# A two-layer transformer on one core: first recurrent products inside the expert merge, and gelu in two buffer pairs

## The reference, cut to what matters

```python
y = ys[dest] * flat_w[order][:, None]            # two experts for each token
xl = xl + gt2 * segment_sum(y, tok)              # the merge, layer 0
hl = modulate(rmsnorm(xl, norm_g[1, 0]), sh1, sc1)
yl, ul = split(hl @ w_in + b_in, 2)              # the recurrent mixer, layer 1
ul = centred_dwconv(ul, conv_w, conv_b)          # 4 taps along the positions
for d in range(2):                               # both directions
    r, ig = sigmoid(ul @ w_gate[d, 0] + ..), sigmoid(ul @ w_gate[d, 1] + ..)   # block-diagonal, 4 blocks
    log_a = LRU_C * r * log_sigmoid(lam[d])
    h_d = scan(exp(log_a), sqrt(-expm1(2 * log_a)) * ig * ul)
out = (gelu(yl) * (h_0 + h_1)) @ w_o + b_o
```

## Time and profile before

| | us |
|---|---|
| median of 3 runs | 2863.82 |
| the profiled execution, as timed | 2864.9 |
| its span in the trace | 2863.1 |
| merge, from the first gather to the last copy | 1578.8 to 1658.4 |
| recurrent stage, first product to the projection's first | 1664.8 to 2082.5 |
| TensorE busy | 2596.7 (91% of the span) |
| VectorE, ScalarE, POOL busy | 1089.8, 858.5, 476.7 |

### The profile page before, as it was taken

How to read it: one execution, slowest core, us unless ns; L and a number is a source line. 1 busy time by engine, 2 the same in 40 slices (tenths; PEclk the granted TensorE clock), 3 DMA queues, 4 the chain that set the end, 5 groups by cost and what they waited for, 6 DMA issues and landing times. The chain is left out here.

```text
span 2863.1 us, 68691 instructions
## 1 busy us (share of the span) xinstructions
PE 2596.7 (91%) x28050; PEld 1802.8 (63%) x28051; DVE 1089.8 (38%) x2482; ACT 858.5 (30%) x1860; POOL 476.7 (17%) x590
## 2 busy tenths in 40 slices
PE   7999999999899689999999489999999599999990
PEld 6888788887645357777776344444445477777770
DVE  3234433443553622222222636556465322222225
ACT  3222322232310023333333514334310133333333
POOL 0111211121221022222222300000010122222222
PEclk9999999999999789999999589999999699999995
DMA  6323223232533397999998610000233799999995
GB/s 255 118 95 112 102 95 120 84 111 73 215 134 139 140 413 313 416 416 395 416 416 327 208 60 30 29 29 29 89 133 125 320 410 417 416 417 416 416 376 180
DMA packets 128661, 644.58 MB, mean 225 GB/s; under 512 B 18865, under 2 KB 31441, under 8 KB 72609
## 3 DMA queue, kind: packets, MB, share of 16 engines
q1 hardware_dynamic: 94912, 540.05, 47.7%
q0 software_dynamic: 17984, 57.16, 5.6%
q10 hardware_dynamic: 15648, 45.71, 4.1%
HBM read 578.29 MB, written 64.57 MB: 225 GB/s over the span
## 5 line engine op out<-in xcount | busy, mean ns | idle before, releaser
L1362 PE MATMUL PS<-wt,xT 128*32 128x256 f32 x13056 | 751.5, 381 | 32.2 <-DVE xT L1500 19.1
L1362 PEld LDWEIGHTS PS<-wt,xT 128*32 128x32 f32 x13056 | 512.4, 110 | 231.8 <-issue 40.6
L1377 PE MATMUL PS<-wt,hidT 128*32 128x256 f32 x6528 | 395.2, 379 | 3.5 <-ACT y L1270 3.5
L1270 ACT ACTIVATE y<-PS 32x256 f32<-32x256 f32 x816 | 305.6, 375 | 304.4 <-PE PS L1377 295.7
L1500 DVE STREAM_TRANSPOSE xT<-xg 128x256 f32<-128x256 f32 x206 | 91.8, 446 | 670.1 <-PE PS L1362 653.7
L1377 PEld LDWEIGHTS PS<-wt,hidT 128*32 128x32 f32 x6528 | 256.7, 110 | 99.4 <-issue 4.4
L719 PE MATMUL PS<-hT,slab 128*128 128x256 f32 x1280 | 295.3, 385 | 6.3 <-DVE low L612 3.5
L719 PEld LDWEIGHTS PS<-hT,slab 128*128 128x128 f32 x1280 | 239.3, 192 | 42.6 <-issue 6.5
L432 POOL TENSOR_SCALAR prob<-prob,inv 128x640 f32<-128x640 f32 (+2 forms) x80 | 130.1, 1626 | 661.3 <-DVE inv L627 661.3
L1218 POOL DMA_INDIRECT xg<-h_d,ib x212 | 207.6, 979 | 166.8 <-POOL ib L1215 166.8
L510 ACT ACTIVATE prob<-prob,low 128x640 f32<-128x640 f32 (+2 forms) x160 | 117.6, 735 | 300.3 <-DVE low L612 300.2
(11 more groups left out here) (234 smaller groups left out, 2637.7 us busy)
## 6 DMA issues: line engine op xcount, KB each, us to landing
wt<-in_w SPq DMA_DIRECT2D x256, 1024.0 KB
wt<-in_w2s SPq DMA_DIRECT2D x128, 1024.0 KB
aw<-in_ada_w SPq DMA_DIRECT2D x48, 1024.0 KB, 5.1
ys_d<-y ACTq DMA_DIRECT2D x204, 128.0 KB
slab<-in_slabs SPq DMA_DIRECT2D x24, 512.0 KB, 3.4
tab<-in_tables SPq DMA_DIRECT2D x8, 1408.0 KB, 7.2
ys_d<-zero POOLq DMA_DIRECT2D x4, 2560.0 KB, 9.5
x_d<-x_p ACTq DMA_DIRECT2D x18, 512.0 KB, 5.0
```

Of the source, the lines that this page charges most:

```text
L1270: ins = a.activation(y[rows, q * QD:q * QD + QD], PS[STRIP * q:STRIP * q + STRIP, DOWN, 0:QD], ACT.Copy)
L1362: mm = t.matmul(PS[32 * g:32 * g + 32, UP, 0:QD], xT[:, k * 32:k * 32 + 32], wt[b][:, q, c * 1024 + g * QD:c * 1024 + g * QD + QD], start= ...
L1377: mm = t.matmul(PS[32 * g:32 * g + 32, DOWN, 0:QD], hT_[:, k * 32:k * 32 + 32], wt[b][:, q, c * 1024 + g * QD:c * 1024 + g * QD + QD], sta ...
```

## The change

1. In the recurrent stage `y2` and `yb` become two buffers each, one for each half. `gelu_in(b,o)` waits for the `close` two halves back, and for half 1 the tanh moves behind `gates(b,1,0)`. The loops over b are written out, with fixed indices. Waits and semaphore increments that only served the loops go.
2. Block 0's product of `wu` leaves the recurrent stage and is made in the merge, over pairs of tiles: after an odd tile n TensorE multiplies both halves with the 256 columns of tiles n-1 and n. `SA` and `SB` are collected there, so that the turns have only PSUM banks 6 and 7, one pair.
3. The copies to `hT` are shared anew. An even tile is copied by both engines, four blocks each; an odd tile by ScalarE alone, eight blocks. VectorE's copies of an even tile stand behind the `norm` of the next tile.
4. `x2` gets a third buffer, and ScalarE touches Sqrt once ahead of the first `weigh`.
5. `wu`, `wy` and `wg` of block 0 are loaded when the slot of the last expert but one is free. The five small vectors are loaded right after the twelve loads of the first experts, and the constants of lambda are made on ScalarE and VectorE ahead of the first item; so are `scol` and `gcol`.

The last merge moves into a class `MergeEnd` with the same instructions, apart from a first Sqrt as in 4.

```diff
+            def into_third(self, sp):                        # MergeMid; expert 30's slot is free
+                self.lru.load_wu(sp, 0)
+                self.lru.load_wy(sp, 0)
+                self.lru.load_wg(sp, 0)
+            def before_items_vector(self, v):
+                v.wait_ge(self.vec_in, 80)
...
+                once(v.tensor_scalar(flat(r.bg), flat(r.bg), 0.5, None, ALU.mult))
+            def evac(n):                                     # ScalarE
+                a.wait_ge(self.tr_ok, n + 1)
+                for k in range(KD if n % 2 else KD // 2):
+                    ins = a.activation(self.hT[:, k, n * P:(n + 1) * P], banks(6, 2)[:, k * P:(k + 1) * P], ACT.Identity,
...
+            def turn(n):                                     # TensorE
+                t.wait_ge(self.dg_ok, 2 * n + 2)
+                t.wait_ge(self.eva_ok, n)
+                t.wait_ge(self.evv_ok, (n + 1) // 2)
+                for k in range(KD):
+                    mm = t.matmul(banks(6, 2)[:, k * P:(k + 1) * P], self.x2[n % 3][:, k * P:(k + 1) * P], self.diag[n % 2][:, :],
...
+            def product(n):
+                t.wait_ge(self.eva_ok, n + 1)
+                t.wait_ge(self.evv_ok, (n + 2) // 2)
+                cols = slice((n - 1) * P, (n + 1) * P)
+                for o in range(2):
+                    for k in range(KD):
+                        t.matmul(banks(3 * o, 3)[:, cols], self.lru.wu[:, k, o * P:(o + 1) * P], self.hT[:, k, cols],
+                                 start=(k == 0), stop=(k == KD - 1))
+            turn(0)
+            t.wait_ge(self.lru.wu_in, 16)
+            for n in range(NT):
+                if n + 1 < NT:
+                    turn(n + 1)
+                if n % 2:
+                    product(n)
...
+            for n in range(NT):                              # VectorE
+                if n + 1 < NT:
+                    add(n + 1)
+                norm(n)
+                if n % 2:
+                    evac(n - 1)
@@ experts, SP @@
+                    merge.early_loads(sp)                    # the five vectors, behind 12 weight loads
                     sp.wait_ge(tab_ok, 1)
@@ recurrent, ScalarE @@
-                            a.wait_ge(z_ok, n + 1)
-                            a.activation(yb[:, :], banks(6, 2), ACT.Identity, bias=bin_[:, 0, k]).then_inc(y_ok, 1)
+                        if n >= 2:
+                            a.wait_ge(z_ok, n - 1)
+                        a.activation(yb[o][:, :], banks(6, 2), ACT.Identity, bias=r.bin[:, 0, k]).then_inc(y_ok, 1)
...
+                        gelu_in(b, 1)
+                        gates(b, 1, 0)
+                        gelu_tanh(b, 1)
+                        gates(b, 1, 1)
@@ recurrent, TensorE @@
+                    t.sem_inc(u_ps, 2)
+                    for b in range(LB):
+                        if b:
+                            t.wait_ge(r.wu_in, 16 * b + 16)
...
+                            product(wu, 1, SB, N, u_ps)
```

More of the change, by code:

```diff
@@ L51 @@
 LW = 1024
+CONV = 4
 LB = 4
@@ L1079, in experts @@
+        def experts(l, nt, w_in, merge):
             dst, w01 = tabs
             NA = 2 * nt
-            last = hT is None
             small = Place(nc, SMALL_AT, RING_AT)
@@ L1128, in experts @@
             passed, sp_passed = nm("passed"), nm("sp_passed")
-            nm = lambda s: sem(f"{s}_c{l}")
-            ys_ok, cols_in, cols_ok, rows_in, x_in = nm("ys_all"), nm("cols"), nm("cols_ok"), nm("rows"), nm("x_in")
-            turned = nm("cols_turned")
-            y_in = [gather_sem(f"y_in{j}_c{l}") for j in range(2)]
-            x_out = [nm(f"x_out{j}") for j in range(2)]
-            ya_ok, s_ok, m_ok, x2_ok, sum_ok, sqrt_ok = (nm(x) for x in ("ya", "ysum", "gated", "x2", "sum", "sqrt"))
-            rs_ok, dg_ok, tr_ok, eva_ok, evv_ok, ob_ok = (nm(x) for x in ("rs", "diag", "turned", "ev_act", "ev_dve", "ob"))
+            ys_ok = nm("ys_all")
+            merge.begin(ys_ok, y)
             iot, tok = cst[:, C_IOT:C_IOT + ITEMS], cst[:, C_TOK:C_TOK + nt]
@@ L1325, in _ @@
                     t.matmul(PS[:, 0, 0:w], ltri[:, :], flat(A2), start=False, stop=True).then_inc(summed, 1)
-                    if not last:
-                        t.wait_ge(cols_in, 48)
-                        t.matmul(PS[:, 5, 0:4 * KD], y[0:4 * KD, 0:P], ident[0:4 * KD, 0:4 * KD], start=True, stop=True
-                                 ).then_inc(turned, 1)
+                    merge.early_tensor(t)
                     e32 = slice(0, EXPERTS)
@@ L1414, in _ @@
                     t.sem_inc(used[5], DEEP - 1)
-                    if not last:
-                        for n in range(nt):
-                            j = n % 2
-                            t.wait_ge(dg_ok, n + 1)
-                            if n >= 2:
-                                t.wait_ge(eva_ok, n - 1)
-                                t.wait_ge(evv_ok, n - 1)
-                            for k in range(KD):
-                                mm = t.matmul(banks(2 * j, 2)[:, k * P:(k + 1) * P], x2[j][:, k * P:(k + 1) * P], diag[j][:, :],
-                                              start=(k % 4 == 0), stop=(k % 4 == 3))
-                            mm.then_inc(tr_ok, 1)
+                    merge.tensor(t)
                 @block.vector
@@ L1520, in _ @@
                             hidden(n)
-                    if not last:
-                        v.wait_ge(turned, 1)
-                        v.wait_ge(cols_in, 48)
-                        for w in range(2):
-                            c = 2 * KD * w
-                            v.tensor_copy(scol[:, w, :], PS[:, 5, c:c + KD]).then_inc(cols_ok, 1)
-                            v.scalar_tensor_tensor(out=gcol[:, w, :], in0=PS[:, 5, c + KD:c + 2 * KD], scalar=1.0, in1=ncol[:, :],
-                                                   op0=ALU.add, op1=ALU.mult).then_inc(cols_ok, 1)
-                        v.wait_ge(cols_ok, 4)
@@ L1551, in norm @@
-                    def norm(n):
-                        j = n % 2
-                        v.wait_ge(sqrt_ok, n + 1)
-                        if n >= 2 and not last:
-                            v.wait_ge(dg_ok, n - 1)
-                        v.reciprocal(rs[:, j:j + 1], rt[:, j:j + 1]).then_inc(rs_ok, 1)
-                        v.wait_ge(rs_ok, n + 1)
-                        if last:
-                            if n >= 2:
-                                v.wait_ge(x_out[j], 16 * (n // 2))
-                            v.scalar_tensor_tensor(out=ob[j][:, :], in0=x2[j][:, :], scalar=rs[:, j:j + 1],
-                                                   in1=fin[:, :], op0=ALU.mult, op1=ALU.mult).then_inc(ob_ok, 1)
-                        else:
-                            if n >= 2:
-                                v.wait_ge(tr_ok, n - 1)
-                            v.tensor_scalar(diag[j][:, :], ident[:, :], rs[:, j:j + 1], None, ALU.mult).then_inc(dg_ok, 1)
@@ L1568, in evac @@
-                    def evac(n):
-                        j, w = n % 2, 0 if n < NTL else 1
-                        v.wait_ge(tr_ok, n + 1)
-                        for k in range(KD // 2, KD):
-                            ins = v.tensor_scalar(hT[:, k, n * P:(n + 1) * P], PS[:, 2 * j + 1, (k - 4) * P:(k - 3) * P],
-                                                  gcol[:, w, k:k + 1], scol[:, w, k:k + 1], ALU.mult, ALU.add)
-                        ins.then_inc(evv_ok, 1)
-                    add(0)
```

902 lines of the change are left out of this document (517 added, 385 removed).

## The result

The changed kernel takes 2823.05 us (median of four runs, 2815.8 to 2824.55) against 2863.42 us for the kernel before: a ratio of 0.985, 95% interval 0.984 to 0.987, or 40 us less. Five further runs of the same kernel, taken later as an experiment, gave 2816.4 us (0.985, 0.983 to 0.986). The nine together do not scatter about one value: five lie from 2815.0 to 2817.1, four from 2822.2 to 2824.6, and none between. That gap turned out to be the most instructive part of the case. The profiled execution took 2824.55 us (span 2822.8), so it is one of the upper group.

What follows compares the result with a forecast made beforehand. TensorE was taken to bound the recurrent stage outside its stops, and the merge to leave it about 3 us free per tile. Terms: -30.2 - 23.5 + 3.5 + 3.0 + 0.5 = -46.7 us, forecast 2817.5 us, range 2808 to 2830.

Steps and rivals of the forecast that it cites:

- Part 1: Recurrent stage, stop before each block's last two gate products: two y2/yb buffers remove four stops, -30.2 us.
- Parts 2 and 3: Merge and recurrent stage's start: wu's product moves into a longer merge; gates start at 1691.9 instead of 1715.4, -23.5 us.
- Part 4: Merge, four TensorE gaps of about 3.0 us: one or two clock falls, +3.5 us, ends 0 and 9.6.
- the dear end: Merge gaps: the clock falls in all four, making the clock term 9.6 us instead of 3.5.
- The first rival: Merge: the clock falls in every gap, +6 us, 2823.5 us; chance 0.15.
- Part 5: Before the first item: VectorE waits for vectors queued behind 12 loads, first item 3.0 us late; ends 0 and 7.
- Part 6: End of the items: loads of wu, wy, wg may share DMA engines with the last store, +0.5 us, ends 0 and 3.
- No stop stayed: Rival, recurrent stage: another wait replaces z_ok and the stops stay, +30 us, 2847.5 us; chance 0.07.
- stay at the low clock: Rival, merge: TensorE stays at 1.2 GHz throughout, merge some 44 us later, 2858 us; chance 0.02.
- the slower case: Rival, expert items: moved loops slow their products; 4.1% growth cancels the gain, 7% gives 2898 us; chance 0.03.

## Why the prediction was right, and where it was not

The forecast was 2817.5 us in a range of 2808 to 2830. The first four runs' median is 2823.05, the median of all nine is 2817.07. The mechanisms of parts 2, 3 and 5 were right and that of part 1 half told; that the sum came so close is in part luck, as the steps show:

**Part 1, -30.2.** Measured -30.3 in the stage and -31.8 with this part alone. The sum was right, its cause only half told. The text gave the stop to the one `y2`/`yb` pair and named the Tanh's place in a subordinate clause. The kernels with one pair and with the Tanh ahead show two edits of about equal worth: with the pair alone the stop is 2.40 us, with the Tanh behind the gates alone 3.08. The tail after the last gates stayed hidden, as costed: the projection follows at 2042.21 without a break.

**Parts 2 and 3, -23.5.** From the merge's first gather to the first gates it was 136.53 us and is 111.12 without falls: -25.4, 1.9 more than worked out (with the falls of part 4 it is 119.86). Putting the product back gives 23.1; that kernel, which keeps the early loads and the third `x2`, takes 134.28 us there, 2.3 less than the kernel before. The walk held: a pair of tiles 13.76 us (1631.87 to 1645.63 in the later run) where 13.8 were worked out; from the second turn to the merge's end 70.45 us against 71.6; the gates 15.8 us after that end against 16.25.

**Part 4, +3.5.** This is the term that was wrong in kind. The text took the gap for one that would cost the clock in one or two places of four. In this kernel's two profiles it was nothing and 8.6 us, near the 9.6 of the dear end (the four gaps themselves cost 7.4, or 1.9 each where 2.4 was reckoned); by their times five runs are of the one kind and four of the other. Three falls of four, in the kernel with the weights behind the columns, show that a gap can go either way by itself. From the earlier trace rows, where the clock fell 2.5 and 3.1 us after the last work, I should have made two outcomes, none and nearly all, and not a mean. The rule of the Trainium skill, "TensorE: Matmul & The Clock Gate", section "Why this matters for your kernels", that gaps of a few microseconds send the clock back, is borne out by the first profile in all four gaps and by the later one in none. The first rival (2823.5) is, by their times, what happened in four runs of nine; 0.15 was too small a chance for it.

**Part 5, +3.0.** Measured +5.8 and +5.2 (37.56 to 43.38 and 42.80), within its ends. The landing of the vectors was estimated as 1017.7, 32.5 us after the first product of the lists; VectorE had them 35.5 and 34.9 us after it (1021.37 and 1019.88). Why they came 2.5 to 3.0 us late is open. SyncE's handing over was slow (the second vector's issue took 6.21 us and the next three 2.14 each), but the last was handed over at 1006.2, long before the weights had landed by the estimate's own 1016.9, so that this alone does not explain it. The DMA engines moved 401 to 434 GB/s from 988 to 1016, as reckoned, and 363 and 379 in the two stretches of 2 us behind that. The same estimate missed what the vectors' place could bring, since it did not see that the weight loads held the columns up too, in the kernel before as well (TensorE waited 6.0 us there); that is where more than a third of the 9.8 us from moving the vectors came from.

**Part 6, +0.5.** From the last product to the first gather 7.78 and 7.53 us against 6.43: +1.35 and +1.1, within the ends. Other kernels with the loads in the same place had from 6.5 to 7.5, and taking them away brought 0.4, so it is a term of 0 to 1.4 us that varies from run to run.

**The sum.** Without any fall the forecast's terms are -30.2 - 23.5 + 3.0 + 0.5 = -50.2, and the later run's span is 50.0 under that of before. But the terms are not those: in the later run they are -30.3, -25.4, +5.2 and +1.1, so that 1.9 us more from parts 2 and 3 made up for most of the 2.8 us that parts 5 and 6 cost too much. With the falls the span is 40.3 us shorter. The forecast's -46.7, with 3.5 us for the clock, stands for neither execution; that it lies beside the median of all nine is luck.

**The other rivals.** No stop stayed (the block takes 96.2 us). The products did not stay at the low clock. The items' products take 750.4 + 395.2 us against 751.5 + 395.2, so the slower case had nothing to stand on.

## What to carry to other kernels

When a stop is ended by one engine's queue, look at every entry between the wait and the instruction that releases the stop: here a second buffer and a Tanh a few places further back brought half each, and either alone left a stop of 2.4 to 3.1 us. Small loads that something waits for go ahead of the big ones, on the same queue (the vectors) and on another (the columns): five vectors of 4 to 16 KB ahead of 12 MB brought 10 us. And where the idle time between two bursts is as long as what the trace has seen cost the clock, forecast the two ends with a chance each, not their mean, and shorten the gap until only the cheap one is left: sharing the copies (1.65 us) took 5 to 14 us off (2810.6 against 2815.8 and 2824.2, the middles of the two groups).

## What the runs showed of the hardware

- The same program with the same idle pieces of 3.04 us lost TensorE's clock in all four in one execution and in none in another, 8.6 us apart; that is most of the difference of their spans (9.7 us), and by the times probably most of this kernel's scatter (2815 to 2825 us). A third execution of the same merge, in another kernel, lost it in three of four. In the two kernels with stops of 2.40 and 3.08 us inside long full-clock work, two of the four stops each were followed by 10.4 to 10.6 us instead of 8.86. The clock can fall after work has begun again: behind the 2.40-us stop that ended at 1746.05 it was 1.00 until 1747 and 0.68 from 1747 to 1748. From the fourth tile on, no turn behind a gap of 1.26 or 1.65 us took over 2.02 us in five profiles. What decides an execution was not tried.
- A 4-KB load took 7.7 us from issue to landing on ScalarE's queue while SyncE issued 1-MB loads at the same moment (changed kernel), and 1.6 to 2.1 us when it was ahead of them (weights behind the columns, vectors first).
- Behind twelve 1-MB loads SyncE's own issue of five small loads took 0.44 us for the first, 6.21 for the second and 2.14 for each of the rest, against 0.33 to 0.43 when they came first.
